# Moving the readout products of the sample states into the middle of the projection tiles of a hybrid decoder layer

## The reference

```python
def gla_recurrent(q, k, v, logd, s0):
    def step(S, inp):
        qt, kt, vt, gt = inp
        S = jnp.exp(gt)[..., None] * S + kt[..., :, None] * vt[..., None, :]
        return S, jnp.einsum('bhd,bhde->bhe', qt, S)

    xs = tuple(a.transpose(1, 0, 2, 3) for a in (q, k, v, logd))
    S, o = lax.scan(step, s0, xs)
    return o.transpose(1, 0, 2, 3), S

p = jnp.einsum('btd,dc->btc', h, w_in).astype(f32)
```

## Time and profile before

| | us |
|---|---|
| median of 3 runs | 2120.32 (2115.84 to 2120.75) |
| profiled execution | 2127.49 |
| its span, from the first to the last instruction | 2125.8 |
| TensorE busy | 1891.1 (89%) |
| VectorE busy | 709.9 (33%) |
| ScalarE busy | 452.2 (21%) |
| GpSimd busy | 275.8 (13%) |

### The profile page before, as it was taken

How to read it: one execution, slowest core, us unless ns; L and a number is a source line. 1 busy time by engine, 2 the same in 40 slices (tenths; PEclk the granted TensorE clock), 3 DMA queues, 4 the chain that set the end, 5 groups by cost and what they waited for, 6 DMA issues and landing times.

```text
span 2125.8 us, 28849 instructions
## 1 busy us (share of the span) xinstructions
PE 1891.1 (89%) x11929; PEld 1241.8 (58%) x11929; DVE 709.9 (33%) x1463; ACT 452.2 (21%) x654; POOL 275.8 (13%) x283
## 2 busy tenths in 40 slices
PE   6598899999598998665968999999999999999998
PEld 2188899897277777435955444444444444444447
DVE  1246644547554434224123222222222212222123
ACT  2143344244222122211222111100110111111012
POOL 1000000101487500204710000000000000000002
PEclk9899999899799999887989999999999999999996
DMA  9943345652865665872532999999999999999991
GB/s 371 402 141 126 119 120 184 212 179 100 326 267 223 239 263 216 313 251 68 176 158 97 420 428 429 428 429 429 429 428 428 428 429 429 429 429 428 429 398 42
DMA packets 123855, 629.14 MB, mean 296 GB/s; under 512 B 10060, under 2 KB 77956, under 8 KB 82295
## 3 DMA queue, kind: packets, MB, share of 16 engines
q1 hardware_dynamic: 118014, 608.45, 71.6%
q0 software_dynamic: 4752, 15.35, 2.1%
q10 hardware_dynamic: 1026, 4.43, 0.6%
HBM read 618.65 MB, written 9.56 MB: 296 GB/s over the span
## 4 chain that ended last, share of the span: by engine, by line
PE 66%; DMA 18%; DVE 5%; ACT 4%; issue 4%; POOL 2%; SPq 0%; DVEq 0%; POOLq 0%; ACTq 0%
DMA ring<-in_w_exp_up 13%; PE pb L2251 13%; PE pb L2259 11%; PE pb L1772 5%; PE pb L2225 5%; PE pb L2043 5%; PE pb L1773 5%; PE pb L1774 5%; PE pb L1705 4%; DMA ring<-in_w_ada 3%; DMA ring<-in_w_ada_final 2%; POOL ring_parts L588 2%; PE pb L2070 1%; PE pb L2231 1%; ACT ring_parts L693 1%
## 5 line engine op out<-in xcount | busy, mean ns | idle before, releaser
L2251 PE MATMUL pb<-ring,pj 128*64 128x512 f32 x2048 | 453.6, 595 | 24.8 <-DMA ring<-in_w_exp_up 14.0
L1772 PE MATMUL pb<-ht_parts,ring_parts 128*128 128x264 f32 x1056 | 313.9, 297 | 22.7 <-POOL ring_parts L588 9.3
L2251 PEld LDWEIGHTS pb<-ring,pj 128*64 128x64 f32 x2048 | 152.2, 137 | 280.8 <-issue 278.3
L1773 PE MATMUL pb<-ring_parts 128*128 128x264 f32 x1056 | 308.1, 292 | 0.0
L1774 PE MATMUL pb<-ring_parts 128*128 128x264 f32 x1056 | 307.7, 291 | 0.0
L1772 PEld LDWEIGHTS pb<-ht_parts,ring_parts 128*128 128x128 f32 x1056 | 208.3, 197 | 31.7 <-POOL ring_parts L588 10.7
L2259 PE MATMUL pb<-ring,pj 128*64 128x512 f32 x1024 | 226.8, 595 | 0.0
L1773 PEld LDWEIGHTS pb<-ring_parts 128*128 128x128 f32 x1056 | 208.4, 197 | 0.1
L1774 PEld LDWEIGHTS pb<-ring_parts 128*128 128x128 f32 x1056 | 207.2, 196 | 0.0
L1705 PE MATMUL pb<-ring,ct 128*32 128x512 f32 x1024 | 147.6, 703 | 63.2 <-DMA ring<-in_w_ada 34.5
L1158 DVE TENSOR_TENSOR ring_parts<-ring,ring_parts 128x2048 fp32r<-128x2048 f32 x50 | 114.6, 2292 | 179.6 <-ACT ring_parts L693 179.6
(11 more groups left out here) (426 smaller groups left out, 2053.9 us busy)
## 6 DMA issues: line engine op xcount, KB each, us to landing
ring<-in_w_exp_gate SPq DMA_DIRECT2D x64, 2048.0 KB, 16.7
ring<-in_w_exp_up SPq DMA_DIRECT2D x64, 2048.0 KB, 17.0
ring<-in_w_exp_down SPq DMA_DIRECT2D x64, 2048.0 KB, 17.2
ring<-in_w_ada SPq DMA_DIRECT2D x48, 2048.0 KB, 8.9
ring<-in_w_in SPq DMA_DIRECT2D x24, 2048.0 KB, 8.0
ring<-in_w_ada_final SPq DMA_DIRECT2D x16, 2048.0 KB, 9.0
ring<-in_w_out SPq DMA_DIRECT2D x8, 2048.0 KB, 8.7
ring<-in_state_gla POOLq DMA_DIRECT2D x8, 512.0 KB, 5.9
```

The lines of the kernel that those rows point to most:

```text
L1772: pe.matmul(out, hi[:, k, :], ht_lo[:, k, :], start=(k == 0), stop=False)
L1773: pe.matmul(out, lo[:, k, :], ht_hi[:, k, :], start=False, stop=False)
L2251: last = pe.matmul(pb[step // 2][SLOT * q:SLOT * q + SLOT, :], xg[:, k, SLOT * q:SLOT * q + SLOT], w[q][:, j, :], start=(k == 0), stop=(k ...
```

## The change

In TensorE's program alone, `in_tile` gets a second argument: a piece of work that is done between the eighth and the ninth of its 16 slices. The readout j is passed to tile 31+j for j from 0 to 6, and outer product 1 to tile 30. The loop then asks for outer product j+2 ahead of tile 31+j. Readout 7 stays between tiles 38 and 39. No other engine's order is changed, and no instruction is added or left out.

```diff
-            def in_tile(t):
+            def in_tile(t, between=None):
...
-                project(pb[m][:, 0:NT], w_hi[:, m], weight_tile(ring_r, in_slot(t), m), as_split=(t == 0))\
-                    .then_inc(S("in_ps"), 1)
+                out, hi, lo = pb[m][:, 0:NT], w_hi[:, m], weight_tile(ring_r, in_slot(t), m)
+                if between is not None:
+                    project(out, hi, lo, 0, 8)
+                    between()
+                    project(out, hi, lo, 8).then_inc(S("in_ps"), 1)
+                else:
+                    project(out, hi, lo, as_split=(t == 0)).then_inc(S("in_ps"), 1)
...
-            in_tile(30)
-            outer(1)
-            in_tile(31)
-            outer(2)
-            pe.wait_ge(*once("gst_evac"))
-            sample_out(0)
-            in_tile(32)
-            outer(3)
-            sample_out(1)
...
-            in_tile(36)
-            outer(7)
-            sample_out(5)
-            in_tile(37)
-            sample_out(6)
+            in_tile(30, lambda: outer(1))
+
+            def state_row(j):
+                outer(j + 2)
+                if j == 0:
+                    pe.wait_ge(*once("gst_evac"))
+                if j == 4:
+                    pe.wait_ge(S("or_evac"), 1)
+
+            for j in range(6):
+                state_row(j)
+                in_tile(31 + j, lambda: sample_out(j))
+            in_tile(37, lambda: sample_out(6))
             in_tile(38)
             sample_out(7)
```

## The result

The changed kernel takes 2145.09 us (median of 4 runs, 2142.80 to 2145.81) against 2120.53 us (4 runs, 2115.84 to 2121.19). The ratio is 1.0119 with a 95% interval of 1.0101 to 1.0136: 24.6 us slower, where 23.7 were forecast. Its profiled execution took 2144.42 us, span 2142.7.

The account below looks back on a forecast made before the run. TensorE was taken as the bound, without idle time from the first outer product to tile 40. The terms 18.2 + 4.2 + 4.7 + 4.7 - 9.3 + 1.2 = +23.7 us gave 2144.0 us from a median of 2120.32; range 2135 to 2151.

Parts of the forecast that it names:

- The wait: TensorE idles before products 2, 4 and 6 until VectorE's keys_apart writes `kz`: 6.08 us each, +18.2 us.
- The clock around the waits: Products 2, 4 and 6 run at 1.2 GHz after idling, 3.33 us for 1.92: +4.2; tiles behind begin low: +4.7.
- The tiles behind them: Tiles behind products 2, 4 and 6 begin at the low clock, 1.55 us each: +4.7 us, bounds 0 and 9.3.
- The products without a wait: Three of outer products 0, 1, 3, 5 and 7 lower the clock: +4.7 us, bounds 0 and 7.8.
- The old stretches: Six 3.4 us stretches at 1.2 GHz in tiles 30 and 32 to 36 are replaced, 1.55 us each: -9.3 us.
- The readout and the clock: The 128-row readout beside an outer product isn't what lowers the clock; moving it away should not save a fall.
- The seams: Places where other work stands between projection matmuls go from 10 to 16, 0.2 us lost at each: +1.2 us.
- `or_evac`: ScalarE's copy of the first four readouts, wanted behind product 6, lies inside the 6.08 us wait: costed at nothing.
- the delay wasn't absorbed: Rival: early loads of `w_ada` behind the projection swallow up to the whole 23.7 us: 2120 to 2124, chance 0.04.
- `kz` wasn't ready: Rival: the readout tips the clock and the next head's keys are ready by tile end: -8.1 us, 2112.2, chance 0.04.
- isolated products did lower the clock twice: Rival judged: outer products apart from readouts no longer lower the clock, the waits stand: +14.8 us, 2135.1, chance 0.08.
- the first rival: Isolated outer products no longer lower the clock; waits stand: 18.2 + 4.7 + 1.2 - 9.3 = +14.8, 2135.1, chance 0.08.

Follow-up runs that it names:

- Experiment 1: The changed kernel with VectorE's keys_apart(1), (2), (3) moved ahead of beside(31), (33), (35): 2120.08 us, ratio 1.0016 to the kernel before.
- experiment 3: The changed kernel with each readout directly behind its outer product, which stays a tile earlier, and no tile split: 2146.18 us, ratio 1.0142.
- experiment 6: The changed kernel with its outer products replaced by 128-row products of other data, not computing the reference: 2135.73 us, ratio 1.0079 to the kernel before.
- experiment 5: The kernel before with its outer products replaced by 128-row products of other data, not computing the reference: 2108.74 us, ratio 0.9959.
- experiment 7: The kernel before with keys and values of the outer products widened from 8 to 128 rows by zeros: 2111.06 us, ratio 0.9982.
- experiment 9: The changed kernel with keys_apart and ScalarE's copy rows_out(0) moved earlier and operands widened to 128 rows by zeros: 2108.94 us, ratio 0.9970 to the kernel before.
- experiment 4: The kernel before with each outer product cut in two, the second half in the middle of the next tile: 2114.59 us, ratio 0.9986.
- experiment 8: The changed kernel with keys_apart and ScalarE's copy rows_out(0) moved earlier, products still 8 rows: 2117.53 us, ratio 1.0010 to the kernel before.
- experiment 2: The kernel before with readouts 0 to 6 moved into the middle of tiles, outer products left where they were: 2117.97 us, ratio 1.0002.

## Why the prediction was right, by its steps

**The wait.** Forecast 3 x 6.08 = 18.2 us, measured 3 x 6.02, by the instruction named and at the products named. Experiment 1 takes it away and the loss goes; experiment 3 has it without the split tiles and keeps the loss. This step is shown.

**The clock around the waits.** The products were taken at 3.33 us and took 3.70: the ratio of 1.73 came from a row at 0.55, and at 0.50 throughout it is 1.93. So +5.4 in place of +4.2. The tiles behind them lost 1.5, 1.6 and 2.2 us to 14, 16 and 22 matmuls at 0.22 us, and 0.2 us in a readout: 5.5 us for the 4.7 forecast. The slow seams and the hand-over at the waits add 0.7 us that I had not priced. The Trainium skill (TensorE: Matmul & The Clock Gate, "Why this matters for your kernels") has gaps in matmul work as what takes the clock away. The 128-row products of experiment 6, slow behind each gap, agree: 3.22 us from start to start in place of 1.54. The falls behind 8-row products, with TensorE busy throughout, have a second cause: they went with the depth (experiments 5, 7 and 9).

**The products without a wait.** Three falls of five were forecast, two came (behind 1 and 5): +3.1 for +4.7.

**The old stretches.** Six of 1.55 us go, -9.3, in these two executions. As the price of a typical execution that was probably too high. Four kernels without a fall in their traces give an estimate: how far their median lies below that of the kernel before, put right by how much their stretch differs from 94.93 - 9.3 = 85.6 us, the stretch of before without falls. Experiment 7 gives 7.7 - 1.9 = 5.8 us, not quite four falls; experiment 4 gives 4.2 + 3.1 = 7.3, experiment 5 gives 7.5, experiment 9 gives 7.9. The recorded ratio of experiment 7, 0.9982, would make it 1.9 us, so the figure is rough. For the order of the changed kernel, experiments 8 and 9 give 8.6 us in the medians, less 86.82 - 83.76 = 3.1: 5.5 us. So the term of the old falls was too large by these estimates, and how many falls a typical execution of either kernel has is open.

**The readout and the clock.** "Moving it away should not save a fall" stands as far as the times reach: experiment 2 is at 1.0002, and the estimates above, 5.8 to 7.9 us with the readouts in the order of before and 5.5 with them apart, are not told apart by such figures. How often a separate product lowers the clock isn't settled: two of five in the changed kernel, four of eight in experiment 2, two of seven without a wait in experiment 1, none of eight in experiment 8, in one profiled execution each. What is shown is that the falls don't need the readout next to the product (experiment 2) and do need the shallow rows (experiments 5, 7 and 9).

**The seams.** +1.2 us was right in size for 8-row products: without falls the stretch of before would take 85.6 us, and that of experiment 8 took 86.8.

**`or_evac`.** Costed at nothing because it lay under the wait for the keys; it did. With that cover gone it cost 1.54 us and a slow tile (experiment 1), ahead of tile 35 and not, as forecast, at a readout.

**The sum.** 18.1 + 5.4 + 5.5 + 3.1 - 9.3 + 1.2 + 0.7 = 24.7 us, against 24.6 measured in the stretch. The mechanism was right. That the forecast came within 1 us is luck in part: the products, the tiles behind them and the hand-over were 2.7 us more than forecast, and one fall fewer took 1.6 back. By the rivals: the delay wasn't absorbed, `kz` wasn't ready, and isolated products did lower the clock twice. The sum of the first rival, +14.8, left out the slow products behind the waits, which don't hang on it; with the 4.2 us it is +19.0.

## What to carry to other kernels

When work is moved on one engine, look in the other engines' order for the instruction that feeds it: a product asked for one tile earlier, while its operand is written behind an evacuation of that same tile, waits for the whole chain, here 6 us for what was free before. Price such a wait with the clock: three waits of 6.0 us cost 27 us in all (experiments 5 and 6). And where TensorE loses its clock while it is busy, look at the depth of the operands; filling up with rows of zeros kept the clock here and shortened the product too.

## What the runs showed of the hardware that I had not expected

A product of depth 8 took 1.92 us from start to start where one of depth 128, of the same columns, took 1.82 us with a readout behind it and 1.54 us with a tile behind it (experiments 5, 7 and 9). Up to the second matmul of the tile behind it the shallow one takes 2.14 us and the deep one 1.85. The deeper one is the cheaper, apart from the clock.

Zeros did as well as data: the granted clock was 1.00 through the stretch with rows 8 to 127 all zero (experiment 7) and with query values in them (experiment 5).

One trace doesn't give the number of falls. The executions of one kernel are far apart: 2106.34 to 2132.17 us with 8-row products and no waits (experiment 8), and the fastest is the one that was profiled. Nor does the spread say where falls are: experiment 9, with rows of zeros in the same order, went only from 2107.01 to 2113.59, but experiment 7, with rows of zeros too, from 2105.51 to 2119.17, and experiment 1, with 8-row products and a wait, from 2117.50 to 2125.26, twelve each.
